# Two heads' value products side by side in TensorE, short and long tiles in pairs, and a staggered first norm, in a two-layer decoder kernel

## What is computed

```
h = rmsnorm(x, g_pre);  x = x + w * rmsnorm(f(h), g_post)
ffn:      f(h) = (silu(h @ wg) * (h @ wu)) @ wd                      # 1024 -> 2816 -> 1024
layer 0:  8 NSA heads of 64 (compressed, selected and window branch, each with its gate) in 2 key/value groups,
          8 DSA heads of 64 that share one key and one value and attend to the 128 best keys of an indexer
layer 1:  8 latent-attention (MLA) heads, 64 + 32 features of keys, values of 64,
          4 differential heads, softmax1 - lambda * softmax2, values of 128
head:     p = softmax(mask(q @ k.T * scale + bias));  o = p @ v      # tiles of 128 queries, keys 0 .. end of the tile
```

## Time and profile before

| | |
|---|---|
| median of 3 runs | 2308.64 us (2307.94 to 2309.53) |
| the profiled execution, its own time | 2309.05 us |
| its span in the profile | 2307.1 us |
| PE busy | 2220.2 us, 96% |
| DVE, ACT, POOL busy | 1245.1, 541.6, 1368.7 us |
| first feed-forward unit work on PE | from 12.5 us |
| NSA and DSA attention | 515.5 to 666 us |
| MLA attention | 1714.3 to 1769 us |

### The profile page before, as it was taken

The page is one execution under the profiler, slowest core; times in us unless marked ns, Lnnn a source line. Parts: engine busy times, 40 slices in busy tenths (PEclk is TensorE's granted clock), DMA queues, the critical chain, the costliest instruction groups (busy, mean ns, idle before and its releaser), DMA issues.

```text
span 2307.1 us, 32871 instructions
## 1 busy us (share of the span) xinstructions
PE 2220.2 (96%) x11594; PEld 1872.1 (81%) x11598; DVE 1245.1 (54%) x2369; ACT 541.6 (23%) x1313; POOL 1368.7 (59%) x850
## 2 busy tenths in 40 slices
PE   7999999999999899999999999999999999999997
PEld 5888888778878788888888888888767879888886
DVE  5554324798876565552256454126577666654323
ACT  2101002318741441100030000004346144101000
POOL 5666666681247466666658666666441755766662
PEclk9999999999999999999999999999999999999998
DMA  5433332310024123333323333333221311333331
GB/s 194 172 91 100 93 93 89 124 55 20 29 92 119 55 65 100 100 92 94 97 74 110 97 94 94 94 92 99 69 69 36 112 58 63 108 92 100 92 93 53
DMA packets 62418, 206.14 MB, mean 89 GB/s; under 512 B 6831, under 2 KB 9263, under 8 KB 61924
## 3 DMA queue, kind: packets, MB, share of 16 engines
q1 hardware_dynamic: 55312, 187.86, 27.1%
q10 hardware_dynamic: 6996, 16.82, 2.2%
HBM read 201.98 MB, written 8.70 MB: 91 GB/s over the span
## 4 chain that ended last, share of the span: by engine, by line
PE 85%; DVE 10%; issue 2%; ACT 2%; POOL 1%; DMA 0%; another core or an unknown queue 0%; SPq 0%; DVEq 0%; POOLq 0%; ACTq 0%
PE bank L784 25%; PE bank L786 25%; PE bank L785 25%; PE bank L1061 3%; PE bank L1044 2%; PE bank L1028 2%; DVE h_lo L1706 1%; DVE ev_logit L1893 1%; DVE top L1990 1%; DVE bank L1767 1%; PE bank L812 1%; DVE x_res L1775 1%; DVE h_lo L1781 0%; DVE h_lo L1929 0%; PE bank L836 0%
## 5 line engine op out<-in xcount | busy, mean ns | idle before, releaser
L635 POOL TENSOR_TENSOR w_lo<-w_raw,w_hi 128x1024 fp32r<-128x1024 f32 (+1 forms) x358 | 866.8, 2421 | 29.9
L784 PE MATMUL bank<-h_hi,w_hi 128*128 128x512 f32 (+1 forms) x2136 | 802.1, 376 | 29.5 <-DVE h_lo L1706 12.2
L633 POOL TENSOR_SCALAR w_hi<-w_raw 128x1024 fp32r<-128x1024 f32 (+1 forms) x358 | 381.3, 1065 | 708.1 <-PE bank L786 537.9
L785 PE MATMUL bank<-h_lo,w_hi 128*128 128x512 f32 (+1 forms) x2136 | 793.6, 372 | 0.0
L786 PE MATMUL bank<-h_hi,w_lo 128*128 128x512 f32 (+1 forms) x2136 | 793.3, 371 | 0.0
L784 PEld LDWEIGHTS bank<-h_hi,w_hi 128*128 128x128 f32 x2136 | 404.7, 189 | 109.5 <-DVE h_lo L1706 12.6
L786 PEld LDWEIGHTS bank<-h_hi,w_lo 128*128 128x128 f32 x2136 | 404.7, 189 | 69.5
L785 PEld LDWEIGHTS bank<-h_lo,w_hi 128*128 128x128 f32 x2136 | 405.0, 190 | 66.9
L784 PE MATMUL bank<-act_hi,w_hi 128*128 128x512 f32 (+1 forms) x792 | 290.1, 366 | 0.0
L785 PE MATMUL bank<-act_lo,w_hi 128*128 128x512 f32 (+1 forms) x792 | 289.4, 365 | 0.0
L786 PE MATMUL bank<-act_hi,w_lo 128*128 128x512 f32 (+1 forms) x792 | 289.4, 365 | 0.0
(11 more groups left out here) (277 smaller groups left out, 2415.0 us busy)
## 6 DMA issues: line engine op xcount, KB each, us to landing
w_raw<-in_w_up SPq DMA_DIRECT2D x176, 512.0 KB, 3.6
w_raw<-in_w_down SPq DMA_DIRECT2D x64, 448.0 KB, 3.3
w_raw<-in_w_down SPq DMA_DIRECT2D x32, 512.0 KB, 3.5
w_raw<-in_w_ev_in SPq DMA_DIRECT2D x19, 512.0 KB, 3.6
w_raw<-in_w_xkv SPq DMA_DIRECT2D x16, 512.0 KB, 3.6
w_raw<-in_w_od_in SPq DMA_DIRECT2D x16, 512.0 KB, 3.6
bias_line_rows<-bias_lines ACTq DMA_DIRECT2D x1, 6400.0 KB
ev_strip<-bias_line_rows ACTq DMA_DIRECT2D x16, 256.0 KB, 3.0
```

The costliest lines, as they stand in the source:

```text
L633: pool.tensor_scalar(w_hi[j][:, 0:cols], raw[j][:, 0:cols], 1.0, 0.0, ALU.mult, ALU.add).then_inc(hi_split, 1)
L635: pool.tensor_tensor(w_lo[j][:, 0:cols], raw[j][:, 0:cols], w_hi[j][:, 0:cols].bitcast(F32), ALU.subtract).then_inc(split_done, 1)
L784: pe.matmul(out, w_hi[j][:, w], hi, start=first, stop=False)
L785: pe.matmul(out, w_hi[j][:, w], lo, start=False, stop=False)
```

## The change

It has three parts.

1. **Column halves.** The value columns are now the 64 features of the head alone. A job of head group 0 (or an even head) writes PSUM rows 0 to 63, its partner rows 64 to 127. The partner jobs stand next to each other in the list (`pair` 0 and 1), and the value products of both are issued in one go, at the step of the first, alternating block by block. PE waits there for the turned probabilities of the second job as well. The padded copies of the values and their zeroing fall away, and MLA now leaves PSUM once for two heads (4 chunks, not 8).
2. **Order of the jobs.** In layer 0 the lengths come as 1, 4, 2, 3 (short with long) in place of 1, 2, 3, 4. In MLA the two heads of a chunk alternate tile by tile.
3. **First norm.** The gains are loaded from ACT's queue, the other constants after `x`; ACT's table is loaded by an early small activation. ACT writes each high part twice, first into PSUM (for DVE), then into `h_hi`; the squares come after all eight chunks, into PSUM too. PE starts the four units staggered: unit `k` takes chunk `t - FIRST_LAG[k]` at step `t`.

```diff
 LAG = (0, 0, 2, 5)
+FIRST_LAG = (0, 3, 5, 7)
+FIRST_SUMS, FIRST_TURN = 9, 11
...
-        for i in range(NT):
-            even += [("cmp", f, i), ("slc", f, i), ("win", f, i), ("slc", f + 4, i), ("win", f + 4, i)]
-    even += [("dsa", h + e, i) for h in range(0, B_HEADS, 2) for i in range(NT) for e in range(2)]
+        for short in range(NT // 2):
+            lengths = (short, NT - 1 - short)
+            even += [("cmp", f, i) for i in lengths]
+            even += [(kind, h, i) for kind in ("slc", "win") for i in lengths for h in (f, f + 4)]
+    even += [("dsa", h + e, i) for h in range(0, B_HEADS, 2) for short in range(NT // 2)
+             for i in (short, NT - 1 - short) for e in range(2)]
...
-    mla = [("mla", h, i) for h in range(C_HEADS) for i in range(NT)]
+    mla = [("mla", h + e, i) for h in range(0, C_HEADS, 2) for i in range(NT) for e in range(2)]
...
-                     v=[v_pad[b][g][:, j, :] for j in range(i + 1)],
+                     v=[ev_v[:, b, j, DH * g:DH * g + DH] for j in range(i + 1)], pair=g,
...
-                     v=[mla_v[:, j, P * (h // 2):P * (h // 2) + P] for j in range(i + 1)],
+                     v=[mla_v[:, j, DN * h:DN * h + DN] for j in range(i + 1)], pair=h % 2,
...
-                pe.wait_ge(split_done, 1)
-                for c in range(KC):
-                    pe.wait_ge(lo_done, c + 1)
-                    mm = product(0, 0, c, h_hi[:, c, :], h_lo[:, c, :], c == 0, c == KC - 1)
+                for t in range(KC + FIRST_LAG[-1]):
+                    for k in range(R):
+                        c = t - FIRST_LAG[k]
+                        if not 0 <= c < KC:
+                            continue
+                        if k == 0:
+                            pe.wait_ge(hi_done, c + 1)
+                            pe.wait_ge(lo_done, c + 1)
+                        if c == 0:
+                            pe.wait_ge(split_done, k + 1)
+                        mm = product(k, k, c, h_hi[:, c, :], h_lo[:, c, :], c == 0, c == KC - 1)
...
-                    for b, v in enumerate(info["v"]):
-                        mm = pe.matmul(bank[B_O[chunk % 2]][features, tokens], v,
+                    pe.wait_ge(probT_copied, jobs[-1]["turn"] + 1)
...
+                    for b in range(last + 1):
+                        for job in jobs:
+                            mm = pe.matmul(bank[B_O[chunk % 2]][job["out"][1], tokens], job["v"][b],
...
+            def first_norm_parts():
+                for c in range(KC):
+                    copy = bank[(B_STAT, B_RT)[c % 2]]
+                    act.wait_ge(x_in[c], 16)
+                    if c >= 2:
+                        act.wait_ge(lo_done, c - 1)
+                    g = G_PRE + c
+                    act.activation(copy[:].bitcast(F32R), x[:, c, :], ACT.Copy, scale=gains[:, g:g + 1]).then_inc(first_hi, 1)
+                    act.activation(h_hi[:, c, :], x[:, c, :], ACT.Copy, scale=gains[:, g:g + 1]).then_inc(hi_done, 1)
...
+                dve.scalar_tensor_tensor(h_lo[:, c, :], x[:, c, :], gains[:, G_PRE + c:G_PRE + c + 1], copy[:],
+                                         ALU.mult, ALU.subtract).then_inc(lo_done, 1)
```

More of the change, by code:

```diff
@@ L374, in build @@
     const_in = sem("const_in")
+    gains_in = sem("gains_in")
+    first_hi = sem("first_hi")
     x_in = [sem(f"x_in{c}") for c in range(KC)]
@@ L440, in kind_of @@
         s = dict(blocks=i + 1, rows=P, w=w, mask=None, k_lo=None, scale=-DH ** -0.5)
-        s.update(opens=True, closes=True, turns=True)
+        s.update(opens=True, closes=True, turns=True, pair=None)
         if kind == "cmp":
@@ L459, in kind_of @@
             s.update(q=q_st[g % 4][:, q], k=k_st[4][0][:, 0:w], k_lo=k_st[4][1][:, 0:w], strip=g,
-                     v=[v_pad[2][h % 2][:, j, :] for j in range(i + 1)],
-                     parts=[(0, w, ev_strip[g % 4][:, off:off + w], None)], opens=h % 2 == 0, closes=h % 2 == 1,
-                     out=(4 + h // 2, slice(0, P), q), mask=taken_mask[:, i - 1, 0:w] if i else None)
+                     v=[ev_v[:, 2, j, 0:DH] for j in range(i + 1)], pair=h % 2,
+                     parts=[(0, w, ev_strip[g % 4][:, off:off + w], None)],
+                     out=(4 + h // 2, slice(DH * (h % 2), DH * (h % 2) + DH), q),
+                     mask=taken_mask[:, i - 1, 0:w] if i else None)
         elif kind.startswith("diff"):
@@ L492, in build @@
             info["ends"] = after != info["out"][0]
[L494 to L498, removed]
+            if infos is INFO[0]:
+                info["opens"] = n == 0 or infos[n - 1]["ends"] or (info["pair"] == 1 and infos[n - 1]["opens"])
+                info["closes"] = info["ends"] or (info["pair"] == 0 and n + 2 == len(infos)) or (
+                    info["pair"] == 0 and infos[n + 2]["out"][0] != info["out"][0])
     fill_of, fill_end, n_fill = [], {}, 8 * OD_FIRST
@@ L723, in k_low @@
             def k_low():
-                for k, n in enumerate(K_ORDER):
+                for n in range(4):
                     pool.wait_ge(k_hi_done, 2 * n + 2)
@@ L1049, in output @@
                     info = infos[s]
-                    if not info["turns"]:
+                    if not info["turns"] or info["pair"] == 1:
                         return
-                    t = info["turn"]
+                    jobs = infos[s:s + 1] if info["pair"] is None else infos[s:s + 2]
                     chunk, features, tokens = info["out"]
-                    pe.wait_ge(probT_copied, t + 1)
+                    pe.wait_ge(probT_copied, jobs[-1]["turn"] + 1)
                     if chunk >= 2 and info["opens"] and tokens.start == 0 and features.start == 0:
@@ L1475, in output_leaves @@
                     else:
-                        rows, chunk = out_rows(phase, f)
-                        act.activation(h_hi[rows, chunk, :], src[rows, :], ACT.Copy).then_inc(hi_done, 1)
+                        act.activation(h_hi[:, f, :], src[:], ACT.Copy).then_inc(hi_done, 1)
                 for s in range(len(infos) + OUT_AT + 1):
@@ L1926, in low @@
                     f = infos[s]["out"][0]
-                    rows, chunk = out_rows(phase, f)
                     dve.wait_ge(hi_done, SPLIT[OUT_KEY[phase]] + f + 1)
-                    dve.tensor_tensor(h_lo[rows, chunk, :], bank[B_O[f % 2]][rows, :], h_hi[rows, chunk, :].bitcast(F32),
+                    dve.tensor_tensor(h_lo[:, f, :], bank[B_O[f % 2]][:], h_hi[:, f, :].bitcast(F32),
                                       ALU.subtract).then_inc(lo_done, 1)
```

104 lines of the change are left out of this document (46 added, 58 removed).

## The result

The changed kernel takes **2295.94 us** (median of 4 runs, 2292.63 to 2296.66), before 2308.64; the ratio is 0.9942, 95% interval 0.9926 to 0.9957, so 12.7 us faster. I forecast 2281: the direction is right, and less than half of the forecast gain came. The profiled execution took 2295.27 us with a span of 2293.2, 13.9 less than before.

What follows compares the result with a forecast made beforehand. PE was taken to bound attention, DVE close behind, and to starve in the first norm. Norm -11.2 and attention -16.5 (NSA -6, DSA -5.5, MLA -5) took 2309.05 to 2281.4, as a median 2281 us; range 2268 to 2299.

Steps and rivals of the forecast that it cites:

- First norm: At the start, where PE starves: faster operands and staggered units gain 11.2 us (9.5 to 13), unit 3 done at 37.5.
- Column halves on PE: Attention value products: 640 instructions at 0.061 us instead of 0.111, 32 us less, before 18 us for entries and exits.
- Rival 1: Value products: the halves don't overlap and the drain is paid, giving 2320 us; chance 0.08.
- Net on PE: -14 us: Attention: column halves' saving less entry costs, of which NSA has 7 us, DSA and MLA 3.5 each.
- rival 3: Attention falls toward DVE's busy time, DVE taking over at its floor: 2268 us, 2262 to 2270; chance 0.07.
- The new wait: PE's pair output waits for the partner's copy by ACT: 2.4 us in NSA, 1 in DSA, 0.5 in MLA.
- The order: Short tiles with long ones even out PE and DVE load, taking back 1.5 us in NSA and 3 in DSA.
- MLA: MLA attention: 5 us less, from halves (-3.5), the wait (+0.5) and dropped ACT copies and DVE subtractions (-2).
- rival 2: Attention: PE waits for ACT at most pairs and gains nothing, leaving 2297 us, 2291 to 2303; chance 0.17.
- waits of PE for ACT's line: Sign to check: PE's waits for ACT's L1464 about 4 us in all; 15 or more would mean rival 2.

Runs made afterwards that it cites:

- e1: Kernel before the change with only the new first norm (staggered units, PSUM copies, reordered loads), attention untouched: 2296.86 us.
- e4: Changed kernel with token tiles back in ascending order 0, 1, 2, 3, pairs still adjacent: 2309.97 us.
- e8: Changed kernel with ascending lengths and a pair's value products issued one step later, with a fourth probability buffer: 2302.73 us.
- e5: Changed kernel with NSA's and DSA's padded 128-column value products back, unpaired, in short-long order; MLA as changed: 2290.33 us.
- e2: Changed kernel with a pair's value products issued one step later, at the second head's step, with a fourth probability buffer: 2289.48 us.
- e10: Kernel of e5 (padded products, short-long order) with turn and output one step later: 2288.48 us.
- e12: Changed kernel with turn at step 5 and output at 7, output still with the first head's step: 2297.34 us.
- e6: Kernel of e2 with the turn one step later too (turn at 5, output at 7) in NSA, DSA and MLA: 2281.53 us.

## Why the prediction was right in sign and wrong in size

NSA and DSA, first logit to memory's sums, in one table (us; in brackets PE's busy and idle time and the clock):

| | padded, own copy | pairs, partner's copy one step back | pairs, two steps back |
|---|---|---|---|
| ascending, turn at 4 | e1: 173.1 (159.5 + 13.6; 0.98) | e4: 187.1 (165.7 + 21.4; 0.89) | e8: 175.0 (155.7 + 19.3; 0.93) |
| short-long, turn at 4 | e5: 165.9 (156.8 + 9.1; 0.98) | changed: 172.9 (152.7 + 20.2; 0.97) | e2: 165.4 (150.6 + 14.8; 0.96) |
| short-long, turn at 5 | e10: 159.8 (154.3 + 5.5; 0.99) | e12: 170.3 (148.0 + 22.3; 0.97) | e6: 155.3 (143.6 + 11.7; 0.99) |

From e1 to the changed kernel, by way of e5 and e2: order -7.2, halves -0.5, new wait +7.5, sum -0.2. I had -4.5, -10.5, +3.4.

1. **First norm, right.** Predicted -11.2 (9.5 to 13), measured -12.1 in time and 36.2 us for the end of unit 3, where I took 37.5. `h_lo` and POOL's second unit (11.22 + 3.5 = 14.7, forecast 14.5) were as worked out. The extra us: full clock came near 14.5, not at 17.3 or later. PE had been at work since 8.89, with the bias-table matmuls (L1297) ahead of the products, which my sum left out; that they brought the clock forward is likely, but no run leaves them out. They start only when the last of ACT's small loads lands, at 8.84; that load, and not POOL, sets PE's start now.
2. **Column halves on PE, right.** 0.054 us each for 0.061; PE's busy time falls by 10.7 us in NSA and DSA at equal clocks (e10, e6) for 10.5 forecast. Rival 1 is out. The 0.061 itself was partly luck: the row that I took it from (L1143) has 62 columns of data where a value product has 128, so it would show that pace without any overlap; only the row halves spoke for one.
3. **The step that failed: "Net on PE: -14 us" put into the sum as if PE's work were the time.** My own windows had DVE at 123.4 of 150.5 us, and nearly all of PE's waits were for DVE's probabilities. What PE saves it spends in good part waiting for the same probabilities, or for ACT's copies: of the 10.7 us of work taken away 5.7 come back as idle time with the turn four steps after its logit (e5, e2), 6.2 with five (e10, e6). The stage wins 0.5 and 4.5 us; the 4 us between them lie in PE's busy time, where e2's clock was lower, and whether its longer waits (up to 1.9 us) lowered the clock or chance did stays open. I had rival 3's floor for DVE as far off, and did not ask how soon PE feels DVE.
4. **"The new wait", mis-sized, 3.4 for 7.5 us.** I counted the copy's 0.6 us after the transposes. It also stands behind an exponential, and that behind DVE (the timeline above). A chunk of NSA has at least three such waits (0.54, 0.23, 0.69), not two of 0.4. In e12, where the other wait is relaxed, it takes 15 us.
5. **The order, mis-sized the other way,** 7.2 us for 4.5 in NSA and DSA. It also keeps the clock: with pairs in ascending order PE's busy time is 13 us longer (e4).
6. **MLA, wrong: -5 forecast, none found.** PE's busy time fell by 3.1 us against e1 (69.75, 66.62), as counted, and the dropped ACT copies show (45.84, 42.83), but PE waits more. Its waits in the changed kernel's MLA:

```profile
PE bank L1047 <- DVE od_prob L1930: 4.8, 6, 1.5
PE bank L1066 <- ACT od_probT L1476: 1.9, 3, 1.0
```

and in e1's, the only one that the view lists:

```profile
PE bank L1050 <- DVE od_prob L1942: 3.2, 6, 1.0
```

The dropped copies show nothing in the time; ACT is busy for 57% of this window (42.83 of 75.3 us), so they probably lay on no path. Without the pair's wait MLA takes 73.7 us at the same clock of 1.00 (e8), 0.7 less than e1's. No run isolates the halves in MLA, so how its share splits stays open.

What happened is rival 2's outcome (2297, 2291 to 2303; chance 0.17) and its mechanism for the larger part: by e2 the pair's wait ate 7.5 us. But it ate what the order had won; of the halves' own gain more than half was lost to PE's waits for DVE and ACT. So "waits of PE for ACT's line", about 4 us by forecast and 15 or more for rival 2, came out between: 8.0 and 1.9.

## What to carry to other kernels

Where PE and another engine are both busy for 80% of a stage or more, work taken from PE is not time won: here some 6 of 10.7 us came back as idle time of PE, so price the change by the waits that it lengthens, not by busy time. Where two waits are in series, remove both: the later output gave 6.5 us, the later turn nothing, both together (e6) 14.4. And when two jobs are joined in one group, the group waits for the younger one's chain: issue it at the younger one's step, and read on the timeline what stands ahead of the last copy in its own engine's queue. A mean clock in the stage's window belongs beside each stage length, or a clock change is read as a gain, as in MLA here.

## What the hardware showed that I had not expected

- Two column halves run at the full rate of both (0.054 us for an instruction of 128 columns, 0.109 in each half) when the instructions alternate. When they don't, only short groups keep that rate: 8 instructions took 0.67 us in turn and 0.66 alternating, 16 took 1.58 and 1.09.
- Which jobs stand next to each other moved the granted clock of a 170 us stage from 0.97 to 0.89, with PE busy for nearly 90% of it in both; the same matmuls took 13 us more of PE's busy time.
